# Even-layer attention loop: all key transposes of a map at the end of a step, value products of two duos together in each fourth step

## The reference, cut to what matters

```python
def diff_attend(q, k, v, lam):
    s = jnp.einsum('bqhmd,bkhmd->bhmqk', q, k).astype(jnp.float32) * (A_QK ** -0.5)
    p = jax.nn.softmax(s, axis=-1)
    a = p[:, :, 0] - lam * p[:, :, 1]
    return jnp.einsum('bhqk,bkhd->bqhd', a, v.astype(jnp.float32))
```

## Time and profile before

| | us |
|---|---|
| median of 3 runs | 1255.57 (1253.93 to 1256.4) |
| the profiled execution | 1254.67 |
| its span, first to last instruction | 1252.9 |
| PE busy | 1222.0 (98%) |
| DVE, ACT, POOL busy | 673.4, 625.2, 461.4 |

### The profile page before, as it was taken

The page is one execution under the profiler, slowest core; times in us unless marked ns, Lnnn a source line. Parts: engine busy times, 40 slices in busy tenths (PEclk is TensorE's granted clock), DMA queues, the critical chain, the costliest instruction groups (busy, mean ns, idle before and its releaser), DMA issues.

```text
span 1252.9 us, 19557 instructions
## 1 busy us (share of the span) xinstructions
PE 1222.0 (98%) x7148; PEld 989.4 (79%) x7148; DVE 673.4 (54%) x1294; ACT 625.2 (50%) x1338; POOL 461.4 (37%) x360
## 2 busy tenths in 40 slices
PE   7999999999999999999999999999999999999997
PEld 5877777777788878988878788787878888777786
DVE  4576974766403344757465756624715700655353
ACT  6544235665532455733366666636336512755543
POOL 5544353222353645521332333232352323222351
PEclk9999999999999999999999999999999999999999
DMA  6331442101432623240435322212263321222443
GB/s 238 110 109 67 175 162 101 35 35 35 152 101 70 233 98 106 100 152 1 146 136 199 136 92 102 102 35 86 83 218 130 123 101 67 86 84 68 169 126 110
DMA packets 28574, 140.33 MB, mean 112 GB/s; under 512 B 4321, under 2 KB 5729, under 8 KB 16001
## 3 DMA queue, kind: packets, MB, share of 16 engines
q1 hardware_dynamic: 21728, 117.72, 26.8%
q10 hardware_dynamic: 6752, 21.35, 5.1%
HBM read 122.74 MB, written 6.29 MB: 103 GB/s over the span
## 4 chain that ended last, share of the span: by engine, by line
PE 77%; DVE 11%; ACT 6%; issue 3%; POOL 2%; DMA 1%; ACTq 0%; DVEq 0%; POOLq 0%; SPq 0%
PE psum L663 47%; PE psum L803 5%; PE psum L693 5%; DVE arena L2370 2%; PE psum L845 2%; DVE small L2367 2%; PE psum L1078 2%; PE psum L942 2%; PE psum L651 2%; POOL w_low L1265 2%; PE psum L1062 1%; PE psum L1054 1%; PE psum L1204 1%; PE psum L1221 1%; PE psum L923 1%
## 5 line engine op out<-in xcount | busy, mean ns | idle before, releaser
L1265 POOL TENSOR_TENSOR w_low<-w_raw,w_high 128x512 fp32r<-128x512 f32 x256 | 348.7, 1374 | 630.2 <-ACT w_high L1453 629.4
L1453 ACT CAST w_high<-w_raw 128x512 fp32r<-128x512 f32 x256 | 153.9, 622 | 255.5 <-PE psum L663 166.9
L663 PE MATMUL psum<-x_high,w_high 128*128 128x512 f32 x528 | 219.7, 416 | 3.5 <-DVE x_low L2207 1.0
L663 PE MATMUL psum<-x_high,w_low 128*128 128x512 f32 x528 | 206.5, 391 | 0.0
L663 PE MATMUL psum<-x_low,w_high 128*128 128x512 f32 x528 | 206.3, 391 | 0.0
L663 PEld LDWEIGHTS psum<-x_high,w_high 128*128 128x128 f32 x528 | 99.7, 189 | 31.7 <-issue 11.6
L663 PEld LDWEIGHTS psum<-x_high,w_low 128*128 128x128 f32 x528 | 99.1, 188 | 21.6
L663 PEld LDWEIGHTS psum<-x_low,w_high 128*128 128x128 f32 x528 | 99.7, 189 | 16.7 <-issue 1.2
L663 PE MATMUL psum<-w_high,x_high 128*128 128x512 f32 x224 | 88.4, 395 | 0.8 <-POOL w_low L1265 0.6
L663 PE MATMUL psum<-w_high,x_low 128*128 128x512 f32 x224 | 87.3, 390 | 0.0
L2585 DVE TENSOR_REDUCE small<-psum 128x1 f32<-128x768 f32 (+1 forms) x96 | 70.0, 771 | 32.1 <-PE psum L1054 31.9
(11 more groups left out here) (486 smaller groups left out, 2789.0 us busy)
## 6 DMA issues: line engine op xcount, KB each, us to landing
w_raw<-stream SPq DMA_DIRECT2D x97, 1024.0 KB, 4.9
x_kept<-arena ACTq DMA_DIRECT2D x8, 512.0 KB, 4.5
arena<-x_kept ACTq DMA_DIRECT2D x8, 512.0 KB, 6.4
arena<-bias ACTq DMA_DIRECT2D x8, 512.0 KB, 4.2
q_masked<-e_q_high SPq DMA_DIRECT2D x24, 96.0 KB, 2.5
arena<-x SPq DMA_DIRECT2D x4, 512.0 KB, 5.3
arena<-x ACTq DMA_DIRECT2D x4, 512.0 KB, 5.4
arena<-ctx ACTq DMA_DIRECT2D x4, 512.0 KB, 4.3
```

The costliest lines, as they stand in the source:

```text
L663: mm = pe.matmul(o, l, r, start=(first and n == 0 and kind != "fc"), stop=(last and n == len(passes) - 1))
L1265: pool.tensor_tensor(PLACE[u][1], RAW[:, g % 2, u % 4, :], PLACE[u][0].bitcast(F32), ALU.subtract).then_inc(w_lo, 1)
L1453: act.copy(PLACE[u][0], RAW[:, g % 2, u % 4, :]).then_inc(w_hi, 1)
```

## The change

Each step's transposes (6 for an x step) now stand together at the end of the step, in banks 4 and 5 as a pair. ACT copies them at the start of its next step in one instruction. The value products of two duos stand together in each fourth step, between the two feeding places, into the two halves of one 256-column output in bank 5, and ACT copies them in one instruction, after its exponentials. The modulation rows stand right behind the scores. The number of fed pieces in four steps goes from 3, 3, 4, 6 to 5, 5, 4, 2. Behind the loop the remaining transposes and the last value products stand between other weight units than before.

```diff
-        FEED_E = ((2, 1), (2, 1), (2, 2), (3, 3))
+        FEED_E = ((3, 2), (3, 2), (2, 2), (1, 1))
...
-            def turn_even(s, c):
+            def turn_even(s):
                 pe.wait_ge(sig("e_p"), s + 1)
-                key = ("e", "T", s, c)
-                acc = open_bank(key, 4)
-                for kt in range(c, min(keys_of(s) // P, c + 4)):
-                    mm = pe.transpose(acc[:, P * (kt - c):P * (kt - c) + P], map_place(s, 0)[:, P * kt:P * kt + P], ident)
+                key = ("e", "T", s)
+                acc = open_two(key, 4) if EVEN[s][0] else open_bank(key, 4)
+                for kt in range(keys_of(s) // P):
+                    mm = pe.transpose(acc[:, P * kt:P * kt + P], map_place(s, 0)[:, P * kt:P * kt + P], ident)
                 fills_bank(mm, key)
...
             def values_even(d):
-                pr, n = EVEN[2 * d][1], keys_of(2 * d) // P
-                for hh in range(2):
-                    for c in parts_of(2 * d):
-                        consumed(pe, ("e", "T", 2 * d + hh, c))
+                for duo in (d - 1, d):
+                    for hh in range(2):
+                        consumed(pe, ("e", "T", 2 * duo + hh))
...
                 key = ("e", "O", d)
                 acc = open_bank(key, 5)
...
             for s in range(n):
                 score_even(s)
-                if s >= 3:
-                    turn_even(s - 3, 0)
-                if s >= 5 and s % 2:
-                    values_even((s - 5) // 2)
-                feed("e", pieces, FEED_E[s % 4][0])
-                if s >= 3 and EVEN[s - 3][0]:
-                    turn_even(s - 3, 4)
-                feed("e", pieces, FEED_E[s % 4][1])
                 if s in MOD_AFTER:
                     modulate_whole(*MOD_AFTER[s], 5)
                 if s in TURN_AFTER:
                     turn_row(*TURN_AFTER[s], open_bank(("modT", *TURN_AFTER[s]), 5))
-
+                feed("e", pieces, FEED_E[s % 4][0])
+                if s >= 7 and s % 4 == 3:
+                    values_even((s - 5) // 2)
+                feed("e", pieces, FEED_E[s % 4][1])
+                if s >= 3:
+                    turn_even(s - 3)
...
             pool[0] = APART_E
-            turn_even(n - 3, 0)
             unit("gc", 0, X, C)
-            turn_even(n - 3, 4)
+            turn_even(n - 3)
             unit("gc", 1, X, C)
...
-            def turned_even(s, c):
+            def turned_even(s):
                 d, hh = s // 2, s % 2
                 if d >= 2:
-                    filled(act, ("e", "O", d - 2))
-                key, w = ("e", "T", s, c), min(keys_of(s) - P * c, 512)
-                ps = filled(act, key)
-                frees(act.copy(E_PT[:, 2 * (d % 2) + hh, P * c:P * c + w], ps[:, 0:w]), key)
+                    filled(act, ("e", "O", d - 2 | 1))
+                key, w = ("e", "T", s), keys_of(s)
+                filled(act, key)
+                frees(act.copy(E_PT[:, 2 * (d % 2) + hh, 0:w], PS[:, 4 * 512:4 * 512 + w]), key)
...
             for s in range(n):
-                if s - 1 in MOD_AFTER:
-                    guest_rows(MOD_AFTER[s - 1])
-                if s - 1 in TURN_AFTER:
-                    turned_row(TURN_AFTER[s - 1])
-                if s >= 3:
-                    turned_even(s - 3, 0)
+                if s >= 4:
+                    turned_even(s - 4)
                 exps_even(s, 0)
                 exps_even(s, 1)
-                if s >= 3 and EVEN[s - 3][0]:
-                    turned_even(s - 3, 4)
-                if s >= 5 and s % 2:
+                if s in MOD_AFTER:
+                    guest_rows(MOD_AFTER[s])
+                if s in TURN_AFTER:
+                    turned_row(TURN_AFTER[s])
+                if s >= 7 and s % 4 == 3:
                     values_even((s - 5) // 2)
```

More of the change, by code:

```diff
@@ L450, in build @@
         keys_of = lambda s: S + L if EVEN[s][0] else L
-        parts_of = lambda s: (0, 4) if EVEN[s][0] else (0,)
-        FEED_E = ((2, 1), (2, 1), (2, 2), (3, 3))
+        FEED_E = ((3, 2), (3, 2), (2, 2), (1, 1))
         GRANULE_STEPS = 8
@@ L1074, in values_even @@
                 acc = open_bank(key, 5)
[L1075 to L1079, removed]
+                for duo in (d - 1, d):
+                    pr, n = EVEN[2 * duo][1], keys_of(2 * duo) // P
+                    own = slice(P * (duo % 2), P * (duo % 2) + P)
+                    for kt in range(n):
+                        for hh in range(2):
+                            head = 2 * pr + hh
+                            mm = pe.matmul(acc[64 * hh:64 * hh + 64, own], E_V[:, kt, 64 * head:64 * head + 64],
+                                           E_PT[:, 2 * (duo % 2) + hh, P * kt:P * kt + P], start=kt == 0, stop=kt == n - 1)
                 fills_bank(mm, key)
@@ L1119, in _ @@
             unit("gc", 5, X, C)
-            values_even(n // 2 - 1)
             mean_squares(0)
@@ L1851, in exps_even @@
                 if m == 0 and s >= 4:
-                    filled(act, ("e", "T", s - 4, parts_of(s - 4)[-1]))
+                    filled(act, ("e", "T", s - 4))
                 if m == 1 and s >= 2:
@@ L1858, in exps_even @@
                                      bias=scr(NEGMAX + c), accum_out=scr(ROWSUM + c)), key)
-            def turned_even(s, c):
+            def turned_even(s):
                 d, hh = s // 2, s % 2
                 if d >= 2:
-                    filled(act, ("e", "O", d - 2))
-                key, w = ("e", "T", s, c), min(keys_of(s) - P * c, 512)
-                ps = filled(act, key)
-                frees(act.copy(E_PT[:, 2 * (d % 2) + hh, P * c:P * c + w], ps[:, 0:w]), key)
+                    filled(act, ("e", "O", d - 2 | 1))
+                key, w = ("e", "T", s), keys_of(s)
+                filled(act, key)
+                frees(act.copy(E_PT[:, 2 * (d % 2) + hh, 0:w], PS[:, 4 * 512:4 * 512 + w]), key)
             def values_even(d):
                 x, pr, t, _ = EVEN[2 * d]
-                key, c = ("e", "O", d), P * t if x else S + P * t
+                key, c = ("e", "O", d), P * (t - 1) if x else S + P * (t - 1)
                 ps = filled(act, key)
-                frees(act.copy(E_Q[:, pr, c:c + P], ps[:, 0:P]), key)
+                frees(act.copy(E_Q[:, pr, c:c + 2 * P], ps[:, 0:2 * P]), key)
             def fed_even(s):
@@ L1900, in _ @@
             gate_units = UNITS["gc"]
-            turned_even(n - 3, 0)
+            turned_even(n - 4)
             high(fed["e"][2 * n - 1] + ROOM)
-            turned_even(n - 3, 4)
             high(gate_units[0] + ROOM)
-            turned_even(n - 2, 0)
-            values_even(n // 2 - 2)
+            turned_even(n - 3)
             high(gate_units[1] + ROOM)
-            turned_even(n - 2, 4)
+            turned_even(n - 2)
             high(gate_units[2] + ROOM)
-            turned_even(n - 1, 0)
+            turned_even(n - 1)
             high(gate_units[3] + ROOM)
-            turned_even(n - 1, 4)
             values_even(n // 2 - 1)
@@ L2645, in _ @@
                 conv_from = next(conv)
-            for s, c in ((n - 2, 4), (n - 1, 0), (n - 1, 4)):
-                filled(dve, ("e", "T", s, c))
+            for s in (n - 2, n - 1):
+                filled(dve, ("e", "T", s))
             values, squares_of, roots_of = six_of(E_Q), six_wide(E_SQ), six_wide(E_RS)
@@ L2652, in _ @@
                 for pr in pairs:
-                    for t in own:
+                    for t in own[1::2]:
                         consumed(dve, ("e", "O", (LT + ST) * pr + t))
```

10 lines of the change are left out of this document (4 added, 6 removed).

## The result

The changed kernel takes 1276.24 us (median of 4 runs, 1272.16 to 1276.86), the kernel before beside it 1254.75 (4 runs, 1253.53 to 1256.40). The ratio is 1.0161, with a 95% interval of 1.0149 to 1.0174: slower, as forecast, but by 20 us (by the ratio; 21.5 by the medians) in place of 12, and above the upper end of the range (1273). The profiled execution took 1275.82 us, with a span of 1274.0 and a mean granted clock of 0.993; before it was 1252.9 and 0.998. The four runs of the changed kernel stand in the order of their mean clocks but for the last two: 1272.16 at 0.995, 1275.82 at 0.993, 1276.67 at 0.990 and 1276.86 at 0.991.

What follows compares the result with a forecast made beforehand. PE was taken to bound the loop; 19.9 us of new waits less 4.1 for fewer groups, 3.9 and 0.6 of old waits gave +11.3, so 1267 us median, range 1257 to 1273.

Steps and rivals of the forecast that it cites:

- What bounds the kernel: Even loop: PE is the bound, busy 196.5 of 199.1 us, so each wait of PE is lost in full.
- Transposes together, nothing: Six transposes in one stretch cost PE 0.66 us, the same as 4 + 2 did.
- Half as many groups of value products, -4.1: 24 groups of value products become 12, at 0.34 us each: 4.1 us less.
- Place 1: Steps 7, 19, 31, 43: transposes wait 1.3 us for bank 5; 2.6 us counted for steps 19 and 43.
- Place 2: Steps 7 and 31: scores wait 0.9 us, transposes 3.6 behind POOL's late scaling; 4.5 twice, 9.0 us.
- Place 3: Steps 11, 23, 35, 47: late copies and exponentials, 0.3 twice and 1.4 twice; 3.4 us.
- Place 4: Steps 15, 27, 39: value products wait 0.62 us each for the copy of transposes; 1.9 us.
- Place 5: Modulation rows (steps 10, 34) and turning (20, 36, 44) wait for tied bank 5, 3.0 us; weight waits in 18, 42 unchanged.
- Nothing else changes in DMAs: Claimed the same loads in the same queue, released at the same steps; no time was added.
- The clock: Rival, chance 0.1: clock falls to 1.2 GHz behind the 3.6 us waits, twice, adding 9 us: 1276.
- the old delays of the scores: Loop: scores' existing waits for an exponential to free their bank, 3.9 us in 13 pieces, would go.
- 0.6 saved in the tail: Behind the loop: the transposes' old 0.6 us wait for a copy would go.

Runs made afterwards that it cites:

- a_cast6: The changed kernel with the limit on casts of weight units moved one step later (step 5's two casts go to step 6); 1273.39 us, ratio 1.0148.
- b_mearly: The kernel before with only the modulation rows and their turning moved from the step's end to right behind its scores; 1269.78 us, ratio 1.0112.
- a_mmid: The changed kernel with modulation rows and their turning between the two feeding places instead of right behind the scores; 1268.18 us, ratio 1.0103.
- a_feedold: The changed kernel with the old numbers of fed pieces, 3, 3, 4, 6 in place of 5, 5, 4, 2; 1280.23 us, ratio 1.0199.
- a_fillall: The changed kernel with dummy products ahead of transposes (steps 7, 19, 23, 31, 43, 47) and modulation rows (steps 18, 42); 1270.45 us, ratio 1.0122.
- b_feednew: The kernel before with the new feeding alone, 5, 5, 4, 2 pieces in place of 3, 3, 4, 6; 1268.35 us, ratio 1.0102.
- a_fill: The changed kernel with dummy products ahead of the six transposes, 14 in steps 7 and 31, 5 in steps 19 and 43; 1271.63 us, ratio 1.0136.

## Why the prediction came out as it did

**What bounds the kernel: right.** PE sets the loop's end: its waits and its clock account for the loop, below.

**Transposes together, nothing: right.** In step 20 they start at 718.35 and the scores behind them at 718.92: 0.57, and with the 0.08 at the next start 0.65, where 0.66 was forecast.

```profile
718.35 0.82 PE L1061 MATMUL psum<-squares_sb,arena 128*128 128x128 f32 x6
718.92 0.94 PE L1053 MATMUL psum<-b_both,q_masked 96*128 96x512 f32 x4
```

**Half as many groups of value products, -4.1: right in size, as far as rows show it.** In the groups by line (618 to 880 us) the idle ahead of their weight loads that no releaser explains went from 3.8 us to 0.4:

```profile
L1079 PEld LDWEIGHTS psum<-arena 128*64 128x64 f32 x448 | 24.4, 137 | 4.3 <-ACT arena L1861 3.2 <-issue 0.4
```

A stretch of 48 takes 2.77 us (727.66 to 730.43), and 0.054 for each product and 0.15 for the group make 2.74.

```profile
727.66 2.84 PE L1079 MATMUL psum<-arena 128*64 128x128 f32 x48
730.43 0.39 PE L692 MATMUL psum<-ctx_high,w_high 128*128 128x256 f32 x1
```

**Place 1, 1.3 us in steps 19 and 43: right.** 1.1 by the row, 1.25 by start to start (709.14 + 0.12 to 710.51).

```profile
710.51 0.85 PE L1061 MATMUL psum<-squares_sb,arena 128*128 128x128 f32 x6 [1.09 <-ACT arena L1867]
```

**Place 2, 4.5 twice: right, in mechanism and size.** The transposes wait 3.5 (3.6 forecast), by the chain through POOL and DVE that was written down; `a_cast6` takes the two low parts out of it, and the wait falls to 1.0. The scores ahead wait 0.9, as forecast. In step 31 they begin 0.6 late, and their second map, whose bank an exponential frees, costs 0.36 more. The list of waits has only 0.34 of that.

**Place 3: right, 3.2 for 3.4.** In steps 11 and 35 the value products and the transposes come 0.4 late together. In steps 23 and 47 the transposes wait 0.7 (0.9 forecast), and the scores ahead lose 0.5 (0.45 forecast):

```profile
725.99 1.31 PE L1053 MATMUL psum<-b_both,q_masked 96*128 96x512 f32 x4
727.13 0.28 PE L692 MATMUL psum<-ctx_high,w_high 128*128 128x256 f32 x1
```

These scores take 1.14, where 0.78 is usual behind six transposes (718.92 to 719.70), and they begin 0.13 late. The list of waits has none of this: it is a weight load that waits 0.42 for the exponential, and this shows in the distances and hardly in PE's idle time.

**Place 4: right.** In steps 15, 27 and 39 the value products wait 2.0 us together by the list of waits, 2.2 from start to start (1.9 forecast).

**Place 5: half right.** The waits for the tied bank are there, 2.5 us from start to start (3.0 forecast): 0.35 for the rows of steps 10 and 34, 0.45 for the turning in 20 and 44, 0.9 in 36. What failed is its last sentence, "In 18 and 42 they wait for their weights as before, about as long", and with it "Nothing else changes in DMAs". In step 18 the load is indeed released at about the same point of the step. But the rows that use it stand 2.25 us of fed products earlier, and I counted that move only against the bank and not against the load. It cost 2.0 us in step 18. The scores of step 4, too, wait for a transfer that they had not waited for (q_masked, 0.15 us idle, 0.5 from start to start). What the move of the rows is worth by itself, 14 us in `b_mearly` and 8 in `a_mmid`, shows that it was the part of the change that deserved the most care; the uneven feeding, with the waits that it makes, hides much of it, which is why taking that table back alone made the kernel slower (`a_feedold`).

**The clock: the mechanism was a rival with 0.1, and it is what happens.** This is the larger failed step. The waits of 3.6 us were forecast, the fall of the clock behind them was priced at 9 us, and it was given a small chance because the earlier trace rows show 1.00 with no wait to try it. It fell in the profiled execution, the mean clocks of the other three runs are about as low (0.990 to 0.995), and it cost 5 to 7 us, not 9: behind both waits of 3.5 us, and once more behind smaller ones, the 1.09 us of step 19 and one of 0.29 behind it:

```profile
712.35 1.25 PE L758 MATMUL psum<-sel_sb,mod_rows 128*128 128x2 f32 x8 [0.29 <-issue]
713.46 0.77 PE L692 MATMUL psum<-x_high,w_high 128*128 128x512 f32 x1
```

The Trainium skill (TensorE: Matmul & The Clock Gate, "Why this matters for your kernels") warns of idle gaps between bursts of matmuls; the traces agree, with 0.93 granted in the stretch around step 31 and 1.00 there in `a_fillall`. An argument that "the trace shows no fall" says nothing where the trace shows no wait of that length either.

**The sum.** From start to start, places 1 to 5 came to 2.5 + 8.9 + 3.2 + 2.2 + 2.5 = 19.3 us where 19.9 were forecast, so the chain of waits was right nearly to the microsecond. 18.2 of these lie inside the loop, up to the start of the last scores; step 47 waits 1.1 more behind them. There, 11 groups of value products less save 3.7, the old delays of the scores that went were 3.3 (and not 3.9), the rows of step 18 cost 2.0 and the scores of step 4 0.5: 18.2 - 3.7 - 3.3 + 2.0 + 0.5 = 13.7. The loop measures 19.0 longer, and the 5.3 between them are what is left for the clock. `a_fillall` says at least 4.7 and the windows at most 6.8. Ahead of the loop the changed kernel has 1.2 us more, on which no part of the change bears. Behind the start of the last scores it has about 1.0 more: the 1.1 of step 47 and 0.9 for the convolution's last pieces (the L650 row), less 0.6 saved in the tail as forecast and 0.3 for the twelfth group; the forecast had the saving and no new wait for the convolution.

So two steps failed. The clock, about 5 us, was left out of the sum as a rival with a chance of 0.1, though the sum itself held the long waits. And the loads of the rows, 2.0 us, were said to be as before. Less these two the measured time would be about 1269, inside the range.

On what the prediction said of bank 5: the six transposes write columns that the pending copy reads, and no run here has them in columns that nothing reads, so which guard the bank would need in that case was not tried.

**Open.** The parts of the change do not add up: alone they cost 13 (feeding), 14 (rows) and 8 us (value products), 35 together, and the change with all of them costs 21. That the feeding, and the waits ahead of the rows, cover the load explains part of it. The clock does not explain it: by the windows 1.7, 5 and 1.7 us were not granted in these three, 8.5 together, and 6.8 in the change, each in its profiled execution. The fourth part, the transposes together in a pair of banks, was not run alone.

## What to carry to other kernels

When a change moves an instruction that waits on a load, count what stood between its release and its use, on every queue: here the rows lost 2.25 us of covering products in one step, and moving them behind the scores cost 14 us alone (`b_mearly`), more than the 4.1 us of saved switches. When a change makes PE wait in a loop where it is otherwise busy, price the wait at its length and again at the clock that may fall behind it, and carry both through the range, since a trace without waits cannot show the second. When waits are added up, look at the distances from start to start as well: a late weight load delays the products behind it and is no idle time of PE. And a group of work that is moved to lie together saves its switches only if the copies on the other side of the shared bank have as much cover as the split groups had.

## What the runs showed of the hardware that I had not expected

- The granted clock falls to 1.2 GHz in a loop in which PE is over 90% busy: behind waits of 3.5 us, and also behind shorter ones: 1.09 and 0.29 us in steps 19 and 20 (709 to 713 us), 1.69 us in `b_feednew`, and 0.75 us at 785 us of `a_fill`. Not at once behind each: behind the 2.45 us wait at 703.88 the fed products still start at full pace.
- Filling the waits with useless products, 60 in all, made the kernel 5 us faster (1270.45 for 1276.24, 4.9 us by the ratios); the change of the pace is 0.43 us from one 512-column product to the next in place of 0.23.
- Which wait is followed by a fall differs between variants, and waits that are removed shift it to others: `a_fill` fills four and has it at 700. It also differs between executions of one kernel: the four of `a_fill` have mean clocks of 0.993 and 0.997, and those with 0.993 take 4 to 5 us longer.
- The weights of the modulation rows are used 4.8 and 5.0 us after their issue in step 18 of the two kernels, where PE waits for them, and 6.3 us after it in step 10 of `a_feedold`, in a stretch where the DMA engines are busy 0.66 of the time. How much of that is the neighbours' doing was not measured.
